# A hybrid decoder block on eight cores: the first x tile goes onto the slab queue in blocks, its squares are summed on TensorE, and later norms are placed by the landing of their tile

## The reference

```python
h = ada_rmsnorm(x, g_ffn1, sh1, sc1)      # rmsnorm(x, g) * (1 + sc) + sh
x = x + 0.5 * gt1 * swiglu_ffn(h, w_ffn1_in, w_ffn1_out)      # 1024 -> 2*2816 -> 1024
h = ada_rmsnorm(x, g_mix, sh2, sc2)
proj = h @ w_in                           # 1024 -> 2048
y_conv = conformer_conv_group(...)        # GLU, causal depthwise conv of 31, layernorm, silu
y_rnn = rglru_group(...)                  # conv of 4, gates, linear recurrence over time
x = x + gt2 * (concat(y_conv, y_rnn) @ w_out)
h = ada_rmsnorm(x, g_ffn2, sh3, sc3)
x = x + 0.5 * gt3 * swiglu_ffn(h, w_ffn2_in, w_ffn2_out)
return ada_rmsnorm(x, g_final, f_shift, f_scale)
```

## Time and profile before

| | us |
|---|---|
| median of 3 runs | 2374.32 |
| the runs | 2369.19, 2374.32, 2564.76 |
| profiled execution | 2375.25 |
| its span, slowest core (7) | 2373.7 |
| spans of cores 0 to 7 | 2363.0, 2348.4, 2352.5, 2371.6, 2357.4, 2371.9, 2354.5, 2373.7 |
| TensorE / VectorE / ScalarE / POOL busy, core 7 | 2249.8 / 1324.7 / 956.6 / 287.0 |

### The profile page before, as it was taken

How to read it: one execution, slowest core, us unless ns; L and a number is a source line. 1 busy time by engine, 2 the same in 40 slices (tenths; PEclk the granted TensorE clock), 3 DMA queues, 4 the chain that set the end, 5 groups by cost and what they waited for, 6 DMA issues and landing times.

```text
span 2373.7 us, 34088 instructions; the slowest of 8 cores (2348.4 to 2373.7 us)
## 1 busy us (share of the span) xinstructions
PE 2249.8 (95%) x10864; PEld 1006.1 (42%) x10864; DVE 1324.7 (56%) x2131; ACT 956.6 (40%) x1473; POOL 287.0 (12%) x552
## 2 busy tenths in 40 slices
PE   1999998998999899899999999999999999999995
PEld 0444443443444344344444444444444444444442
DVE  5323225524433485674776476487487588477522
ACT  3313213303110533553565536436536556454512
POOL 0011110020000110201110120111111111120000
PEclk9999999999999999999999999999999999999998
DMA  9899798899866685654665665556456566564452
GB/s 258 189 232 215 194 206 214 214 212 243 214 187 164 191 223 170 190 167 141 194 207 158 207 200 191 154 171 227 153 178 214 160 171 222 158 186 138 151 177 89
DMA packets 122704, 446.86 MB, mean 188 GB/s; under 512 B 18864, under 2 KB 19248, under 8 KB 121520
## 3 DMA queue, kind: packets, MB, share of 16 engines
q1 hardware_dynamic: 90864, 330.44, 44.7%
q0 software_dynamic: 31664, 114.23, 21.5%
HBM read 426.87 MB, written 71.30 MB: 210 GB/s over the span
## 4 chain that ended last, share of the span: by engine, by line
PE 85%; DMA 8%; issue 2%; DVE 2%; ACT 2%; POOL 1%; SPq 0%; DVEq 0%; ACTq 0%; POOLq 0%
PE ps L457 83%; DMA sb_x<-x 2%; PE ps L1097 2%; DMA sb_cs<-wmod 2%; DMA sb_fs<-b 1%; DMA sb_fs<-w 1%; DMA sb_hidB<-wmod 1%; DMA sb_cs<-bm 1%; DVE sb_rstdm L441 1%; DMA x<-sb_x 0%; SPq L417 0%; POOL sb_urep L1087 0%; ACT sb_hb L434 0%; POOL sb_x L417 0%; ACT sb_ntmp L434 0%
## 5 line engine op out<-in xcount | busy, mean ns | idle before, releaser
L457 PE MATMUL ps<-sb_hb,sb_fs 128*128 128x512 bf16 x5632 | 1245.6, 382 | 35.5 <-DMA sb_fs<-w 14.2
L457 PEld LDWEIGHTS ps<-sb_hb,sb_fs 128*128 128x128 bf16 x5632 | 553.9, 98 | 711.8 <-issue 62.5
L457 PE MATMUL ps<-sb_hidA,sb_fs 128*128 128x512 bf16 x2288 | 505.7, 379 | 0.8 <-DVE sb_hidA L441 0.8
L434 ACT ACTIVATE sb_sgf<-ps 128x512 f32<-128x512 f32 x352 | 206.5, 593 | 406.8 <-PE ps L457 364.3
L457 PEld LDWEIGHTS ps<-sb_hidA,sb_fs 128*128 128x128 bf16 x2288 | 223.9, 98 | 269.6 <-issue 1.3
L441 DVE TENSOR_TENSOR sb_hidA<-ps,sb_sgf 128x512 bf16<-128x512 f32 x286 | 195.4, 688 | 227.1 <-PE ps L457 161.4
L457 PE MATMUL ps<-sb_hb,sb_cs 128*128 128x512 bf16 x992 | 224.2, 379 | 4.5 <-DMA sb_cs<-bm 3.4
L1087 POOL DMA_DIRECT2D sb_urep<-sb_ub x256 | 131.0, 520 | 694.5 <-PE ps L457 435.6
L437 DVE SCALAR_TENSOR_TENSOR sb_x<-ps,sb_gth,sb_x 128x512 f32<-128x512 f32 x128 | 96.0, 750 | 174.8 <-PE ps L457 174.4
L434 ACT ACT_TABLE_LOAD x102 | 130.9, 1283 | 154.4 <-PE ps L457 134.1
L437 DVE SCALAR_TENSOR_TENSOR sb_ux<-sb_ub,sb_vecs,sb_ux 128x512 f32<-128x512 bf16 x240 | 179.7, 749 | 10.0 <-DVE sb_ux L437 0.9
(11 more groups left out here) (104 smaller groups left out, 1338.6 us busy)
## 6 DMA issues: line engine op xcount, KB each, us to landing
sb_fs<-b SPq DMA_DIRECT2D x396, 512.0 KB, 4.4
sb_cs<-bm SPq DMA_DIRECT2D x78, 512.0 KB, 4.1
sb_x<-x POOLq DMA_DIRECT2D x96, 256.0 KB, 7.9
sb_cs<-wmod SPq DMA_DIRECT2D x46, 512.0 KB, 12.6
sb_rs<-bm SPq DMA_DIRECT2D x34, 512.0 KB, 5.0
sb_fs<-w POOLq DMA_DIRECT2D x33, 512.0 KB, 9.9
b<-sb_fs SPq DMA_DIRECT2D x33, 512.0 KB, 8.8
b<-w POOLq DMA_DIRECT2D x33, 512.0 KB, 10.3
```

The lines of the kernel that those rows point to most:

```text
L434: return Op(ACT, lambda h: [h.activation(out=out, in_=in_, func=func, **kw)], reads, writes, cost, tset)
L457: out.append(h.matmul(ps[:, bank, :], lhsT=l, rhs=r, start=(first and k == 0), stop=(last and k == n - 1)))
```

## The change

- The first tile (tile 2, buffer `sb_x0`) is loaded in 8 blocks on SP's queue, behind the first four modulation slabs and ahead of the fifth. It was one 2 MB DMA on POOL's queue, issued first. The second tile too is loaded in 8 blocks, on POOL as before.
- The gates move: first weight slab at `order[7]` (was 8), second weight slab at `order[10]` (was 14, with the others), second x tile at `order[12]` (was 11), the others at `order[14]` as before. The second weight slab is now ahead of the second x tile.
- Squares of the first tile go as bf16 to `sb_sqb` and `sb_sqbo` in turn, and eight matmuls with ones sum them in PSUM; VectorE's seven additions are gone.
- The norms of the later tiles of phase 1 are offered only when the model has the tile landed for 30 us (groups 1 and 2) or 12 us (tiles 6 and 7) by TensorE's clock.
- For the first weight slab of the program gate and up matmuls alternate by block instead of 8 and 8.
- Final norm: one `y` semaphore for each tile instead of one for each block, so a tile load waits for all eight `y` stores of its buffer. For the last tile the Exp table is loaded by a tiny activation ahead of block 7, the sum of blocks 0 to 6 goes through a matmul of its own, block 7's squares go straight to a second one, and the stores are on SP's queue.
- `CVD`, `CVP` and the loops over them spell the conv channels out; their values give the same operations.

```diff
         r_start = RL(3)
...
-                    fplan.append(load_cast(w1_d[s], [r_start[min(s, 1)]]))
+                    fplan.append(load_cast(w1_d[s], [r_start[min(s, 2)]]))
...
+                if k == 4:
+                    yield flag(("xl", groups[0][0]))
...
+        def landed(si, margin):
+            return lambda: core.force or PE.clock > max([r.tw for r in r_x[si]]) + margin
...
-                        gate = [r_modr[order[11]]]
-                        yield lambda: r_modr[order[11]].w is not None
-                    if gi == 0:
-                        yield dma(PL, xs[si][:], x_d[t], gate, r_x[si], s_x[si], 2 * MB)
+                        gate = [r_modr[order[12]]]
+                        yield lambda: r_modr[order[12]].w is not None
+                    if t == groups[0][0]:
+                        yield lambda: mload[0] >= 4
+                        yield from xload(si, x_d[t], [], SP, newsem("s_xf"))
+                    elif gi == 0:
+                        yield from xload(si, x_d[t], gate)
...
+                    if gi > 0:
+                        yield landed(si, 30.0 if gi < 3 else 12.0)
                     yield lambda: normlock.take(1)
...
+                        for fc in range(8):
+                            sq, r_sq = ((sqb, r_sqb), (sqbo, r_sqbo))[fc % 2]
+                            yield act(sq[:], xs[si][:, fc, :], AF.Square, [r_x[si][fc]], [r_sq])
+                            yield mm(bank, [(ones_bf[:], sq[:])], [r_sq, r_ones], first=(fc == 0), last=(fc == 7))
...
+                if last:
+                    got = yield lambda: bankM.take(1)
+                    bank = got[0]
+                    for fc in range(8):
+                        if fc == 7:
+                            yield mm(bank, [(ones_bf[:], sqbo[:])], [r_sqbo, r_ones], last=False)
+                            yield act(sgm[:, 0:1], hstate[:, 0:1], AF.Exp, [r_hst[0]], [r_sgm], tset="E", cost=0.2)
+                        yield flag(("x3c", t, fc))
+                        yield from accum(st, xt[:, fc, :], r_xt[fc], True)
+                    yield mm(bank, [(ones_bf[:], cvb[:])], [r_cvb, r_ones], first=False)
...
-                    yield dma(PL, y_d[t, fc], xt[:, fc, :], [r_xt[fc]], [], s_y[fc], MB // 4)
+                    sy = s_y[t % 4] if not last else s_yl
+                    yield dma(SP if last else PL, y_d[t, fc], xt[:, fc, :], [r_xt[fc]], [], sy, MB // 4)
+                for fc in range(8):
+                    r_xt[fc].r[sy] = sy.val
...
-            for j, kk in ((0, 8), (1, 14)):
+            for j, kk in ((0, 7), (1, 10), (2, 14)):
```

More of the change, by code:

```diff
@@ L92, in __init__ @@
         self.pipe = 0.0
-        self.now = 0.0
+        self.force = False
     def start_of(self, op):
@@ L247, in run_streams @@
                 best = (key, k)
-        assert best is not None, [s.name for s in streams]
+        if best is None:
+            assert not core.force, [s.name for s in streams]
+            core.force = True
+            continue
+        core.force = False
         s = streams[best[1]]
@@ L369, in build_program @@
         s_x1 = [newsem(f"s_xs{k}") for k in range(4)]
-        s_y = [newsem(f"s_y{k}") for k in range(8)]
+        s_y = [newsem(f"s_y{k}") for k in range(4)]
+        s_yl = newsem("s_yl")
         s_fs = [newsem(f"s_fs{k}") for k in range(NFS)]
@@ L697, in accum @@
                 return
+            if split and k == 7:
+                yield act(cvb[:], src, AF.Square, [r_src], [r_cvb])
+                return
             q = nxt(name, 2)
             yield act(sq[q][:], src, AF.Square, [r_src], [r_sq[q]])
-            if k < 7:
+            if split and k == 6:
+                yield add(accb[:], acc[:], sq[q][:], [r_sq[q], r_acc], [r_accb])
+            elif k < 7:
                 yield add(acc[:], acc[:], sq[q][:], [r_sq[q]], [r_acc])
@@ L812, in ffn_in @@
                 bg, bu = got
-                for half, b in ((0, bg), (8, bu)):
-                    if cg == 0:
-                        for kc in range(8):
-                            yield (lambda kc=kc: r_hb[hi][kc].w is not None)
+                if cg == 0:
+                    for kc in range(8):
+                        yield (lambda kc=kc: r_hb[hi][kc].w is not None)
+                        for half, b in ((0, bg), (8, bu)):
                             op = mm(b, [(sl[:, half + kc, :], hbs[hi][:, kc, :])], [r_sl, r_hb[hi][kc]], first=(kc == 0), last=(kc == 7))
                             yield op
-                    else:
+                else:
+                    for half, b in ((0, bg), (8, bu)):
                         op = mm(b, [(sl[:, half + kc, :], hbs[hi][:, kc, :]) for kc in range(8)], [r_sl] + r_hb[hi])
@@ L1086, in fn @@
                     for sft in range(4):
-                        out.append(h.dma_start(out=urep[q][32 * sft:32 * sft + 32, 1 - h2:2, :],
-                                               in_=ub[32 * q:32 * q + 32, 1 + h2:2 * h2 + 2, sft:sft + WU]))
+                        out.append(h.dma_start(out=urep[q][32 * sft:32 * sft + 32, c0 - 2 * h2:2, :],
+                                               in_=ub[32 * q:32 * q + 32, c0:2 * h2 + 2, sft:sft + WU]))
                 return out
-            return Op(PL, fn, [r_ub[2 * h2 + k] for k in range(1 - h2, 2)], [r_urep], dma=s_ur, nbytes=128 * 4 * (1 + h2) * WU * 2, ndma=16)
+            return Op(PL, fn, [r_ub[k] for k in range(c0, 2 * h2 + 2)], [r_urep], dma=s_ur, nbytes=128 * 4 * (2 * h2 + 2 - c0) * WU * 2, ndma=16)
         def conv_mm(b, sl, r_sl, c):
@@ L1127, in c_gen @@
                 bankM.give(bv)
-                if c == 0:
-                    streams.append(Stream(f"V{i}", v_gen(i), dict(b_m, dve=0)))
-                if c == 1:
+                if c in CVD:
+                    streams.append(Stream(f"V{i}.{c}", v_gen(i, c), b_v))
+                if c == 1 and CVP[0] < 2:
                     yield spread(0)
             flags.add(("glu", i))
-            for c in range(1, 4):
+            for c in CVP:
+                if c == 2 and CVP[0] == 2:
+                    yield cring.has(k0 + 4)
+                    cring.done(k0 + 4)
+                    yield spread(1)
                 k = k0 + 4 + c // 2
@@ L1273, in o_gen @@
                 st = stat_o()
-                yield from stats(xt, r_xt, st, before=lambda fc, t=t: flag(("x3c", t, fc)))
-                got = yield lambda: bankM.take(1)
-                bank = got[0]
-                yield total(st, bank)
+                last = t == n_tiles - 1
+                if last:
+                    got = yield lambda: bankM.take(1)
+                    bank = got[0]
+                    for fc in range(8):
[5 more added lines that the diff above has]
+                    yield mm(bank, [(ones_bf[:], cvb[:])], [r_cvb, r_ones], first=False)
+                else:
+                    yield from stats(xt, r_xt, st, before=lambda fc, t=t: flag(("x3c", t, fc)))
+                    got = yield lambda: bankM.take(1)
+                    bank = got[0]
+                    yield total(st, bank)
                 yield rstd_ops(rstd_o, r_ro, bank, 1.0 / D)
@@ L1367, in prep_inputs @@
             shared[:, V_RCW + 4 * cc + k] = rcw[k, cc * 128:(cc + 1) * 128]
-    shared[:, V_CW:V_CW + NCONV] = f(inputs["conv_w"][0])[:, 0:128].T
+    for j, cc in enumerate(CVD):
+        shared[:, V_CW + NCONV * j:V_CW + NCONV * (j + 1)] = f(inputs["conv_w"][0])[:, 128 * cc:128 * cc + 128].T
     def blocks(w, rows, cols):
```

77 lines of the change are left out of this document (44 added, 33 removed).

## The result

The changed kernel took 2386.70 us in the median of 12 runs (2378.79 to 2725.62), beside 2382.74 us for the kernel before on the same chip (12 runs, 2369.19 to 2648.83). The ratio of comparable runs is 1.0036 with a 95% interval of [1.0019, 1.0053], so 8.5 us more (4.5 to 12.6), where 16.8 us less was forecast and the range ended at 2376.

The account below looks back on a forecast made before the run. TensorE, busy 95% of core 7's span, was taken as the bound. Terms 0 - 8.5 - 8 - 1.5 + 4 - 2.8 = -16.8 us took 2375.25 to 2358.5, 2358 for the median; 8-in-10 range 2341 to 2376.

Parts of the forecast that it names:

- Norms of tiles 0 and 6: Phase 1 norms: placed later, they no longer wait 11.37 and 7.61 us for their tiles; -8.5 and -8 us.
- The margin of "27 us, more than 11.37": Norm of tile 0: standing 8 SiLUs later, 27 us, exceeds its 11.37 us wait for its tile.
- Its own sign of being wrong: Stated in advance: waits of VectorE for `wmod` slabs longer than 12.67 us would show the forecast wrong.
- Loads after `y` stores: Mixer tile reloads: last block issued 3.8 us later; one wait reaching 6 us costs 4 us, bounds 0 and 12.
- Tile 7's is covered: Tile 7's load: its norm moves 10 us against an 8.03 us wait, covering what the new semaphore adds.
- Head: Start until both tiles of the first pair are normed: sum 0 us, bounds -5 and +5.
- the gate one slab later is covered by that queue: Second tile's load in the head: its later gate adds nothing beyond the 2.8 us from POOL's queue order.
- Its sign of being wrong, the second tile landing after 60: Head: the second tile landing before 50 or after 60 us would show the forecast wrong.
- Norm of tile 7: Norm moved by 3 SiLUs, 10 us, against an 8.03 us wait: -1.5 us, bounds -1.75 and 0.
- tail: Final norm: addition and table load leave the path, -2.2 us; stores from SP, -0.6; together -2.8 us.
- the stalls come back as DMA waits: Rival, chance 0.20: busy DMA engines make 14 of the 18 us saved return; 2372 us.
- The reloads decide, and it is slower: Rival, chance 0.07: four mixer norms after `y` stores wait over 11 us each, costing 34 us instead of 4; 2388 us.

Follow-up runs that it names:

- with both waits out of the way: Kernel before with norms held back until their tile is in and modulation slab products held back 20 us instead of 8: 0.9952 of the kernel before.
- quarter slabs: The combination with only 256 of the 1,024 columns of each modulation slab loaded from slab 16 on: 0.9908 of the kernel before.
- the combination: Changed kernel with the old head, one semaphore per block of `y` and slab products held back 20 us; held norms and new tail kept: 0.9940 of kernel before.
- the tail alone: Kernel before with only the new final norm of the last tile: 0.9981 of the kernel before.
- held 2.9: Kernel before with only the norms of tiles 0, 6 and 7 held back as in the changed kernel: 1.0012 of the kernel before.
- head 6.4: Kernel before with only the new head: 1.0027 of the kernel before.
- semaphore 17.4: Kernel before with only one semaphore for each tile of `y` in place of one for each block: 1.0073 of the kernel before.
- block semaphores: Changed kernel with one semaphore for each of the eight blocks of `y` again: 1.0021 of the kernel before.

## Why the prediction was wrong, step by step

- **Norms of tiles 0 and 6: the step that failed** (forecast -8.5 and -8, measured +0.5 and -0.9, neither clear of zero). The prediction saw that ScalarE waited for `sb_x`, concluded that the stall would go with that wait, and let VectorE's 12.67 us for a slab "stay" at no cost. The wait for `sb_x` did go, and in the old place it was the one that ended last. But the sum of squares needs ScalarE and VectorE, and VectorE's slabs were late too; in the old place they landed while VectorE stood behind ScalarE. In the new place VectorE's wait ends last. The margin of "27 us, more than 11.37" was compared with the tile's landing and with nothing of what stood on VectorE in the new place. Its own sign of being wrong was waits for `wmod` over 12.67 us. Only one core has one at these norms (14.48 us, core 2 at tile 6; the longest before was 13.27); what did the harm on core 3 were three within 21 us, of 9.49, 5.60 and 10.12. The size was too high as well: with both waits out of the way the stages of tiles 0 and 6 fall by 6.4 and 3.7 us, and with quarter slabs on top (in the combination) by 6.3 and 12.9.
- **Loads after `y` stores** (+4, measured +10 to +12, bounds 0 and 12): right mechanism, wrong size. ScalarE's wait near 1660 grew from 2.37 to 5.62 us, about the 3.8 us of issue that it counted, but TensorE's stage grew by 5.7, and three of the four reloads reached TensorE where it took one. The three stages grew by 11.7 us; undoing the part takes back 9.5 of them in this kernel, and adding it to the combination costs 11.7 in the whole time. "Tile 7's is covered" held, and it covered 5.1 us.
- **Head** (0, measured +5.0 for the same work, bounds -5 and +5): "the gate one slab later is covered by that queue" was wrong; POOL waited 3.80 us for that gate, the tile was issued 3.9 us later and took 2.4 us longer to land. Its sign of being wrong, the second tile landing after 60, came true on four cores (60.73 on core 3) and not on the other four (56.5 to 58.5). The wait for a weight slab that it takes away moved to the next slab. The first square came at 23.38, not 20 to 22.
- **Norm of tile 7** (-1.5, measured -2.0 to -2.8) was right. So was the **tail** (-2.8, measured -3.8 in the profile, -4.5 [-7.4, -1.9] by the tail alone) in its main term: the addition and the table load are worth 2.3 us against 2.2. The stores gave 1.5 instead of 0.6, over the bound of 1.2. The choice of the row's 1.28 us for the table load was borne out.
- The rival "the stalls come back as DMA waits" named the right resource and VectorE's slab, but gave 14 of 18 us back at tile 6, not all of it at tile 0. "The reloads decide, and it is slower" had the right side; it was three tiles at 2 to 6 us, not 34 in all. Neither alone reached the result; together with the head's 5 us they do.
- The parts don't seem to add. One at a time on the kernel before, held 2.9, head 6.4, semaphore 17.4 and tail -4.5 give 22 us, not 8.5; by the intervals of the four the sum is uncertain by 13 us, so the whole times alone don't prove it, and the stages must. Of the 14 us between, 5 are the tile 7 reload that the held norm covers, and about 6 the slab stall at tile 0, which eight cores show with the norm held alone and four in the changed kernel. What spares the other four is open. It isn't a late second tile: the four cores that stall are those whose second tile came latest (first square at 60.7 to 61.6, the others at 56.5 to 58.5). Nor does an early one explain it, since with block semaphores and the same head a core at 60.6 was the only one spared.

## What to carry over

A stall that two engines feed does not go with the wait named last: before moving work off a late transfer, read every in-order engine that the work needs at its new place, and if one of them stands before another transfer there, cost the move at zero until both are moved. Where the DMA engines are as busy as here (0.87 to 0.99 in these stretches), judge a part by stages over all cores and in a two-by-two with its neighbour, since its worth alone (0 and 0) says nothing of its worth in company (11 us). A shared semaphore for several stores costs the landing of the last one and the issue of the rest: at all five reloads behind `y` stores POOL waited 4.0 to 6.0 us ahead of the first block, where it had waited at most 2.3 us ahead of the last (core 3). And check that a stage holds the same work before its times are compared: seven matmuls hid 1.5 us of the head.
